# A two-block transformer kernel in float32: seven and eight slots for the streamed weights, and the expert tables exchanged inside the first expert block

## The reference

```python
logits = (h @ w_router).astype(jnp.float32) + b_router.astype(jnp.float32)
top_val, top_idx = lax.top_k(logits, TOP_K)          # TOP_K = 4 of N_EXPERTS = 32
gates = jax.nn.softmax(top_val, axis=-1)
...
gu = xe @ w_gate_up[e] + b_gate_up[e]                # 1024 x 2048
g = jnp.minimum(gu[:, :D_FF], SWIGLU_LIMIT)
u = jnp.clip(gu[:, D_FF:], -SWIGLU_LIMIT, SWIGLU_LIMIT)
act = (u + 1.0) * (g * jax.nn.sigmoid(SWIGLU_ALPHA * g))
return act @ w_down[e] + b_down[e]                   # 1024 x 1024
```

## Time and profile before

| | us |
|---|---|
| median of 3 runs | 2977.72 (2977.36 to 2981.62) |
| profiled execution, its own time | 2975.44 |
| its span | 2973.6 |
| TensorE matmuls busy | 2833.6 (95%) |
| VectorE busy | 1469.0 (49%) |
| ScalarE / GpSimd busy | 490.3 / 84.3 |
| mean granted TensorE clock | 0.987 |
| weight chunks through the ring | 626, 8.6 us from issue to landing (median) |
| first block begins / last block ends | 277.5 / 1502.6 |

### The profile page before, as it was taken

How to read it: one execution, slowest core, us unless ns; L and a number is a source line. 1 busy time by engine, 2 the same in 40 slices (tenths; PEclk the granted TensorE clock), 3 DMA queues, 4 the chain that set the end, 5 groups by cost and what they waited for, 6 DMA issues and landing times.

```text
span 2973.6 us, 34793 instructions
## 1 busy us (share of the span) xinstructions
PE 2833.6 (95%) x13298; PEld 1904.0 (64%) x13298; DVE 1469.0 (49%) x3187; ACT 490.3 (16%) x989; POOL 84.3 (3%) x111
## 2 busy tenths in 40 slices
PE   4989999999999999999999999999999999999998
PEld 3565454555545454444577768688888867587897
DVE  6764111444442121111267864566664778746666
ACT  1222100122211010000112041121020111311211
POOL 0000000000000000000100001000000000011000
PEclk9989999999999999999999999999999999999999
DMA  8557899999999989999964414522331543134442
GB/s 340 230 211 314 358 401 383 386 396 393 393 397 374 406 344 392 397 400 402 384 226 146 150 51 154 184 101 106 123 125 57 215 180 144 57 142 186 168 170 100
DMA packets 108788, 749.73 MB, mean 252 GB/s; under 512 B 12784, under 2 KB 13168, under 8 KB 21584
## 3 DMA queue, kind: packets, MB, share of 16 engines
q1 hardware_dynamic: 92736, 682.66, 57.9%
q0 software_dynamic: 8816, 50.07, 4.5%
q10 hardware_dynamic: 7072, 14.76, 1.4%
HBM read 737.22 MB, written 10.22 MB: 251 GB/s over the span
## 4 chain that ended last, share of the span: by engine, by line
PE 81%; DMA 10%; DVE 7%; ACT 1%; issue 1%; SPq 0%; DVEq 0%; ACTq 0%
PE ps L650 18%; DMA ring<-stream 9%; PE ps L1384 9%; PE ps L1390 8%; PE ps L884 8%; PE ps L1138 7%; PE ps L975 7%; PE ps L662 6%; PE ps L880 3%; PE ps L1348 2%; PE ps L1336 1%; PE ps L682 1%; PE ps L711 1%; PE ps L985 1%; PE ps L1030 1%
## 5 line engine op out<-in xcount | busy, mean ns | idle before, releaser
L650 PE MATMUL ps<-area,ring 128*128 128x256 f32 x2432 | 532.9, 381 | 0.3
L650 PEld LDWEIGHTS ps<-area,ring 128*128 128x128 f32 x2432 | 464.9, 192 | 65.8 <-DVE area L2358 1.1
L975 PE MATMUL ps<-ring,area 128*64 128x512 f32 x1984 | 449.4, 599 | 34.5 <-DMA ring<-stream 34.0
L975 PEld LDWEIGHTS ps<-ring,area 128*64 128x64 f32 x1984 | 134.0, 137 | 348.4 <-issue 254.3
L884 PE MATMUL ps<-area,ring 128*128 128x256 f32 x1152 | 255.5, 380 | 0.0
L884 PEld LDWEIGHTS ps<-area,ring 128*128 128x128 f32 x1152 | 216.0, 190 | 28.5 <-issue 0.2
L1138 PE MATMUL ps<-ring,area 128*64 128x512 f32 x960 | 214.4, 599 | 4.3 <-ACT area L2936 4.3
L2301 DVE SCALAR_TENSOR_TENSOR area<-area,cols 128x256 f32<-128x256 f32 x480 | 201.8, 485 | 1.1
L662 PE MATMUL ps<-ring,area 128*128 128x512 f32 x448 | 193.7, 592 | 0.0
L1384 PE MATMUL ps<-ring,area 128*128 128x256 f32 x768 | 173.1, 379 | 0.0
L1384 PEld LDWEIGHTS ps<-ring,area 128*128 128x128 f32 x768 | 145.6, 190 | 19.7
(11 more groups left out here) (407 smaller groups left out, 2885.7 us busy)
## 6 DMA issues: line engine op xcount, KB each, us to landing
ring<-stream SPq DMA_DIRECT2D x626, 1024.0 KB, 8.6
area<-shared_modulation POOLq DMA_DIRECT2D x32, 1024.0 KB, 5.5
area<-modulation SPq DMA_DIRECT2D x16, 1536.0 KB, 6.5
expert_rows<-area ACTq DMA_DIRECT2D x62, 128.0 KB, 7.2
area<-stream POOLq DMA_DIRECT2D x4, 1024.0 KB, 15.2
x<-x_tiles ACTq DMA_DIRECT2D x1, 1024.0 KB, 12.7
area<-ctx_tiles ACTq DMA_DIRECT2D x1, 1024.0 KB, 4.8
input_rows<-area ACTq DMA_DIRECT2D x4, 256.0 KB, 8.1
```

Of the source, the lines that this page charges most:

```text
L650: i = mm(ps[:, b, 0:n], w[:, k % 4, j * P:(j + 1) * P], rhs(k), start=(k == 0), stop=(k == 4 * kgs - 1))
L975: i = mm(ps[half(h), bank, :], xT[:, k % 4, half(k // 4)], w[:, 2 * (k % 2) + h, :], start=False, stop=(k == KD - 1))
```

## The change

RING becomes 7, and an eighth slot, `extra`, at 25088 of `area`, holds every eighth chunk from block 2's first on, 42 of them. `selw` moves to 12800. The spill passes keep six slots. The scratch memory of GpSimd's transfers is set to 8192 bytes; before it is the default. Three experts are fixed in place of one; `busiest`, `relabel` and `places` run inside block 0, after its row numbers. SP waits for `flag` before block 3.

```diff
+FIXED = 3
-RING = 6
+RING = 7
+SPILL_RING = 6
+EXTRA_EVERY, EXTRA = 8, 42
+SCRATCH = 8192
...
+EXTRA_FIRST = CH["moe", 2, 0]
+def in_extra(c):
+    n, r = divmod(c - EXTRA_FIRST, EXTRA_EVERY)
+    return r == 0 and 0 <= n < EXTRA
+def extras_before(c):
+    return min(max(-(-(c - EXTRA_FIRST) // EXTRA_EVERY), 0), EXTRA)
+def place_of(c):
+    if in_extra(c):
+        return RING, extras_before(c) + 1
+    n = c - extras_before(c)
+    return n % RING, n // RING + 1
+def _earlier():          # EARLIER[c]: the chunk that held c's slot before
...
-        selw = v(25088, TT, WIDE)
+        selw = v(12800, TT, WIDE)
+        extra = v(25088, 4, 512)
...
             def chunk(c):
                 if c > K.asked:
-                    pe.wait_ge(landed[c % RING], 16 * (c // RING + 1))
+                    pe.wait_ge(*landing_of(c))
                     K.asked = c
-                return ring[:, c % RING]
+                return kept_at(c)
...
             def busiest():
-                V.max(most, counts[:, 1:NE]).then_inc(...)
+                V.max(most, counts[:, FIXED:NE]).then_inc(...)
+                V.tensor_reduce(stat("fixed"), counts[:, 0:FIXED], AX, ALU.max).then_inc(...)
...
                 if scattered:
                     summed(tag, 1)
+                if main and e == 0:
+                    busiest()
+                    relabel()
+                    places()
                 work("A")
...
-            def busiest_then(first):
-                busiest()
+            def rows_first(first):
...
-            busiest_then(first)
+            rows_first(first)
-            relabel()
-            places()
...
             def one(c, d):
-                if c >= RING:
-                    sp.wait_ge(used, c - RING + 1)
-                load(d, c % RING, landed[c % RING])
+                if c == EXTRA_FIRST:
+                    sp.wait_ge(*at((("moe", 0), "chunk", 8)))
+                if EARLIER[c] is not None:
+                    sp.wait_ge(used, EARLIER[c] + 1)
+                sp.dma_start(kept_at(c), stream[d]...).then_inc(landing_of(c)[0], 16)
...
-                if e == 1:
+                if e == FIXED:
                     sp.wait_ge(*at("flag"))
-                if e:
+                if e >= FIXED:
                     own = nc.sync.value_load(order[0:1, e:e + 1], ...)
...
-        nc = bacc.Bacc("TRN2", ..., num_devices=1)
+        nc = bacc.Bacc("TRN2", ..., num_devices=1, dynamic_dma_scratch_size=SCRATCH)
```

More of the change, by code:

```diff
@@ L199, in _plan @@
             if (e, ci) not in SPARE:
-                put(("moe", e, ci), 1, DRAM["moe"] + (e * CPE if e == 0 else 0) + ci)
+                put(("moe", e, ci), 1, DRAM["moe"] + (e * CPE if e < FIXED else 0) + ci)
     for e in range(NBLK, NBLK + 8):
@@ L225 @@
 _plan()
+EXTRA_FIRST = CH["moe", 2, 0]
[10 more added lines that the diff above has]
+def _earlier():
+    held, before = {}, {}
+    for c in range(CH["total"]):
+        s = place_of(c)[0]
+        before[c] = held.get(s)
+        held[s] = c
+    return before
+EARLIER = _earlier()
+assert EXTRA % RING == 0
 COL = {}
@@ L359, in build @@
         mark, at, last = K.mark, K.at, K.last
-        landed = [K.sem(f"weights_landed{s}") for s in range(RING)]
+        landed = [K.sem(f"weights_landed{s}") for s in range(RING + 1)]
         inputs_stored = K.sem("input_rows_stored")
@@ L566, in slots @@
             c = CH["ff1", l, 0] + 2 * i
-            return ring[:, c % RING], ring[:, (c + 1) % RING]
+            return kept_at(c), kept_at(c + 1)
         def weights_of(l, i, p):
@@ L587, in build, with kept_at, landing_of @@
         xn1v = v(B1, KD, SEQ)
-        spill_landed = [K.sem(f"spill_weights_landed{s}") for s in range(RING)]
+        spill_landed = [K.sem(f"spill_weights_landed{s}") for s in range(SPILL_RING)]
+        def kept_at(c):
+            s = place_of(c)[0]
+            return extra if s == RING else ring[:, s]
+        def landing_of(c):
+            s, n = place_of(c)
+            return landed[s], 16 * n
         units_of = {l: [(h, 0) for h in range(H2)] for l in range(LAYERS)}
@@ L962, in expert_chunk @@
                 if wait_it:
-                    base = 16 * (2 * NE * (K.spill_pass) + ci // RING + 1)
-                    pe.wait_ge(spill_landed[ci % RING], K.i * 32 + base)
-                return ring[:, ci % RING]
+                    base = 16 * (2 * NE * (K.spill_pass) + ci // SPILL_RING + 1)
+                    pe.wait_ge(spill_landed[ci % SPILL_RING], K.i * 32 + base)
+                return ring[:, ci % SPILL_RING]
             def half(h):
@@ L1747, in busiest @@
             def busiest():
-                V.max(most, counts[:, 1:NE]).then_inc(*mark("vector_steps"))
+                V.max(most, counts[:, FIXED:NE]).then_inc(*mark("vector_steps"))
+                V.tensor_reduce(stat("fixed"), counts[:, 0:FIXED], AX, ALU.max).then_inc(*mark("vector_steps"))
                 dve.wait_ge(*last("vector_steps"))
-                V.max_index(idx[:, TT, :], most, counts[:, 1:NE]).then_inc(*mark("vector_steps"))
+                V.max_index(idx[:, TT, :], most, counts[:, FIXED:NE]).then_inc(*mark("vector_steps"))
                 dve.wait_ge(*last("vector_steps"))
@@ L1755, in busiest @@
                 TS(stat("over2"), most[:, 1:2], float(CAP), None, ALU.is_gt).then_inc(*mark("vector_steps"))
-                TS(stat("over3"), counts[:, 0:1], float(CAP), None, ALU.is_gt).then_inc(*mark("vector_steps"))
+                TS(stat("over3"), stat("fixed"), float(CAP), None, ALU.is_gt).then_inc(*mark("vector_steps"))
                 dve.wait_ge(*last("vector_steps"))
-                TS(stat("top"), stat("top"), 1.0, None, ALU.add).then_inc(*mark("vector_steps"))
+                TS(stat("top"), stat("top"), float(FIXED), None, ALU.add).then_inc(*mark("vector_steps"))
                 TT_(stat("over"), stat("over1"), stat("over2"), ALU.max).then_inc(*mark("vector_steps"))
@@ L2536, in weight_sums @@
                     for n in (c, c + 1):
-                        dve.wait_ge(landed[n % RING], 16 * (n // RING + 1))
+                        dve.wait_ge(*landing_of(n))
                     if i > 2:
@@ L3197, in one @@
             def one(c, d):
-                if c >= RING:
-                    sp.wait_ge(used, c - RING + 1)
-                load(d, c % RING, landed[c % RING])
+                if c == EXTRA_FIRST:
+                    sp.wait_ge(*at((("moe", 0), "chunk", 8)))
+                if EARLIER[c] is not None:
+                    sp.wait_ge(used, EARLIER[c] + 1)
+                sp.dma_start(kept_at(c), stream[d].rearrange("p (k n) -> p k n", k=4)).then_inc(landing_of(c)[0], 16)
             def load_mod(g):
@@ L3230, in _ @@
                     if (e, ci) not in SPARE:
-                        one(CH["moe", e, ci], DRAM["moe", e, ci] if e == 0 else own * CPE + (DRAM["moe"] + ci))
+                        one(CH["moe", e, ci], DRAM["moe", e, ci] if e < FIXED else own * CPE + (DRAM["moe"] + ci))
             for e in range(NBLK, NBLK + 8):
@@ L3240, in _ @@
                 for ci in range(CPE):
-                    if ci >= RING:
-                        sp.wait_ge(again, ci - RING + 1)
-                    load(DRAM["moe"] + ci, ci % RING, spill_landed[ci % RING])
+                    if ci >= SPILL_RING:
+                        sp.wait_ge(again, ci - SPILL_RING + 1)
+                    load(DRAM["moe"] + ci, ci % SPILL_RING, spill_landed[ci % SPILL_RING])
                 for p in range(NPASS - 1):
@@ L3246, in _ @@
                         for ci in range(CPE):
-                            sp.wait_ge(again, e * CPE + (CPE * NE * p + ci - RING + 1))
-                            load(e * CPE + (DRAM["moe"] + ci), ci % RING, spill_landed[ci % RING])
+                            sp.wait_ge(again, e * CPE + (CPE * NE * p + ci - SPILL_RING + 1))
+                            load(e * CPE + (DRAM["moe"] + ci), ci % SPILL_RING, spill_landed[ci % SPILL_RING])
                 sp.wait_ge(again, CPE * NE * (NPASS - 1))
@@ L3410, in program @@
     def program(known, per):
-        nc = bacc.Bacc("TRN2", target_bir_lowering=False, num_devices=1)
+        nc = bacc.Bacc("TRN2", target_bir_lowering=False, num_devices=1, dynamic_dma_scratch_size=SCRATCH)
         args = [nc.dram_tensor(n, w.shape, F32, kind="ExternalInput").ap() for n, w in arrays.items()]
```

## The result

The changed kernel takes **2931.55 us** (median of 4 runs, 2927.07 to 2933.11), the kernel before 2977.54 on the same chip: ratio 0.9842, 95% interval 0.9829 to 0.9854. That is 47 us faster by the ratio (43 to 51). The profiled execution took 2927.07 us, 48.4 less than the 2975.44 of before.

A forecast was written before the change was run, and what follows sets the result against it. TensorE was taken as the main bound, waiting for weight chunks only in the expert blocks' gate and up products. 2975.4 - 33 (ring) - 0 (exchange) = 2942.4, plus 2.3 for the median: 2945 us, range 2933 to 2962.

The forecast's parts named there:

- where: TensorE waits for weight chunks only in the expert blocks' gate and up products, 34.0 us; layers and start gain nothing.
- the exchange: Expert tables' exchange moved from ahead of block 0 into it: -2.8 - 2.4 + 3.5 + 1.3 = -0.4 us, taken as 0.
- The clock's two terms: TensorE's granted clock: up to 2.4 us back at the expert stage's start, 1.3 us lost after block 0's new wait.
- what a wait costs: In gate and up products, a chunk wait costs 1.4 times its idle time, in sum 47 us over three stretches.
- the carry of the chunks: Chunks of blocks 0 to 31 carried one after another by three rules: the new ring saves 33.5 us.
- second rule: A chunk lands 4.7 us after its load goes out, or 2.48 us plus row traffic's time after the one before.
- the three rules: Load goes out when its slot's chunk is used; landing by the second rule; TensorE takes 1.73 us or the trace's time.
- the ceiling of 40 us: Blocks 2 to 30: each stretch gains at most the smaller of stalls and DMA idle time, 11.9 + 25 + 2.9 us.
- Rival (b): All 47 us of chunk stalls go and the exchange gives 5 us: 2926, from 2926 to 2936; chance 0.12.
- (a): With more loads in flight each transfer takes 1 to 3% longer; 0 to 20 us left, 2958 to 2977; chance 0.14.
- (c): Smaller scratch memory holds one gather of expert rows at a time: 46 us lost, 2991 in all; chance 0.04.
- (d): SP's own waits for the extra slot keep the ring six deep in effect: 2978; chance 0.03.

## Why the prediction was right and wrong

**Right: where.** The waits of the gate and up products went, the layers and the start did not move (at most 1.3 us), and the exchange came out at nothing: the biases start at 274.07 us (said: 274.7), the new wait is 3.15 us (said: 3.5), the exchange ends at 305.3 (said: 306.7). L947 waits for L2031 in place of L985's wait for L2170.

The clock's two terms in that sum were off by 1.8 and 1.3 us in opposite directions, and that they nearly cancelled is luck. Before, the granted clock is 0.50 (1.2 GHz) from 275.3 to 282.1 us, of which TensorE works from 277.49 on, so 4.6 us at half the clock cost 2.3. In the changed kernel it is 0.50 from 274.7 to 278.1, with TensorE busy throughout, and costs 1.7 us: 0.6 came back where 2.4 was put. After the new wait the clock stayed at 1.00 from 300 to 307 us: nothing lost where 1.3 was put. So the sum reads -2.9 - 0.6 + 3.2 + 0 = -0.3, for the -0.4 forecast. In the second profile of the changed kernel the clock did fall around the same wait (0.50 from 311.4 to 314.8 us), and the L947 behind it took 1.12 us for 0.66.

**Right: what a wait costs.** 47 us by 1.4 times the idle time; blocks 2 to 30 became 46.6 us shorter while 31.3 us of waits went, 1.5 times. With five slots it was 62.6 us for 51.1 of waits, 1.2 times.

**Wrong: the carry of the chunks, 33.5 us where 46.6 came.** The step that failed is its second rule. A chunk lands 2.48 us "plus what the gathers and stores of expert rows took there" after the one before: this took lateness read from the trace of six slots and kept it with its chunk in the new ring. That is 86.7 us for all loads but the refills (14.5 + 72.2). With the new ring the same loads are 67.8 us late (4.6 + 63.2). What went was lateness of loads that go out behind two or fewer others, 38.9 us before and 19.3 after; the loads behind three or more kept theirs, 47.8 and 48.5. So part of what the rule called the rows' price was the short queue's. The refills themselves, which the rule let go, gave another 26.7 us (37.6 less 10.9).

How much of the miss is this? I carried the chunks of blocks 2 to 30 once more by the three rules, with TensorE's time for each chunk taken as the shortest in the profiles with seven or more slots (an estimate). With the lateness of the old trace the new ring takes 1063.6 us, 36.9 less than six slots by the same rules; with the lateness of its own trace it takes 1052.8, and 1053.5 was measured. So this one step is worth some 10 of the 13 us that were missing. The 3 us between 36.9 and the prediction's 33.5 lie in how the rules were carried out and are not assigned. The same step put seven slots at 28.9 and the eighth under 5; blocks 2 to 30 have 37.6 (1100.1 less 1062.5) and 9.0.

**Wrong: the ceiling of 40 us,** and with it the lower end of the range, 2933, which was this ceiling and 4 us of exchange. It was the DMA's idle time by its share, with 1.00 as full. The share prints 1.01 when full, and to two places: one hundredth in these 1100 us is 11 us. Length by share, stretch by stretch, gives the DMA engines' busy time with each ring (blocks 2 to 30, us):

```
                      length    busy   idle   TensorE's waits
five slots            1162.7   1069     93    85.1 us, 126 times
six (before)          1100.1   1057     43    34.0,  64
seven                 1062.5   1050     13     9.5,  21
seven and the eighth  1053.5   1050      3     2.7,   6
```

The busy time hardly moves, the idle time is what a slot takes away. So the reading was sound in kind, but coarse: blocks 27 to 30 were capped at 2.9 us and gave 5.8, and blocks 2 to 7 at 11.9 and gave 13.9. By the rates, 387 to 403 of 423 GB/s, the cap would have been 20, 56 and 7 us, above the stalls in the first two stretches, and the sum 13 + 25 + 7 = 45. Rival (b) had the stalls' 47 us and the lowest times; what I held against it, that the idle time ends at 40, rested on this rounding. Its other half, 5 us from the exchange, did not come, and its 2926 stands 5.6 us under the 2931.55.

**The rivals.** (a) The DMA does not slow with more loads in flight: it moves 404 to 414 GB/s where it moved 387 to 403. (c) The smaller scratch memory alone moves the time by nothing that can be seen (0.9995), and in the changed kernel the eight gathers of expert rows go out over 30.8 us and land at most 17.0 us after their issue, where the earlier trace rows have 30.7 and 16.6.

```profile
L3211 POOL DMA_INDIRECT area<-expert_rows,row_at x8: 933/938/1737, 1398.5 to 1429.3; - x8
...
DMA to landing us min/median/max: 5.0/9.7/17.0
```

(d) The eighth slot works as a slot: 9 us of the gain go when it is taken out. The rule of the Trainium skill, DMA: Bandwidth & Descriptors, section Specifications, of 358 GB/s for a core's reads does not bind this kernel: even 414 and 421 GB/s were reached over 220 us.

## What to carry to other kernels

Where TensorE waits for streamed data and the DMA engines look 95% busy, compare their bytes per second with the best short window, not their share with 1.00, and take the waits' full price (here 1.2 to 1.5 times the idle time) as the gain until some rate contradicts it. The loads that gained from more slots here were those that had gone out behind two or fewer others, so a ring should keep three or more loads in flight also while the consumer holds a slot for its longest step (7 us here, for loads 2.48 us apart). Lateness read from a trace with a shallow queue is in part the queue's own and must not be carried over as a price of other traffic. Work moved off the front of a stage is worth something only where its engine's idle time can hold it: the exchange's 10.7 us put behind block 0's last step, ahead of 6.6 and 6.2 us of idle time, gave some 4 us; ahead of the first context step they gave nothing.

## What the runs showed that was not expected

A DMA share of 1.01 is not a full set of DMA engines: with the stores doubled it stayed at 1.01 while the rate rose from 414 to 421 GB/s in the same 222.8 us. Added row traffic of 7.6 MB over blocks 2 to 30 cost 24.8 us with six slots (1124.9 for 1100.1) and 3.4 us with the new ring (1056.9 for 1053.5), each by one pair of profiles. And TensorE's granted clock after the short waits at the start of the expert stage differs between executions of the same instructions by 5 us of lost time, so an edit of a few us there needs many runs, not two profiles.
